# Gathering the routed rows of an expert in float32 by a scaled selection, and using the freed memory for a quarter of a down-projection chunk

## The reference

```python
logits = h2 @ w_router + b_router
top_v, top_i = lax.top_k(logits, 4)
gates = softmax(top_v)
# for each expert e, over the rows (tokens) that chose it:
gu = xb @ w_gate_up[e] + b_gate_up[e]              # 1024 -> 2048
gate, up = minimum(gu[:, :1024], 7), clip(gu[:, 1024:], -7, 7)
act = (up + 1) * gate * sigmoid(1.702 * gate)
yb = act @ w_down[e] + b_down[e]                   # 1024 -> 1024
y[row_tok] += yb * row_g
```

## Time and profile before

| | |
|---|---|
| median of 3 executions | 1183.34 us (1183.27 to 1184.69) |
| profiled execution, its own time | 1185.5 us |
| its span in the profile | 1183.7 us |
| TensorE busy | 1133.4 us, 96% |
| VectorE, ScalarE busy | 381.9 us, 181.8 us |
| mean DMA rate | 375 GB/s over the span |

### The profile page before, as it was taken

One profiled execution on the slowest core, in us unless ns is written; L12 is line 12 of the kernel. 1 busy time (PEld: TensorE's weight loads), 2 busy tenths in 40 slices (PEclk: granted clock), 3 DMA queues, 4 the chain that ended last, 5 costly groups with the idle time before them and its releaser, 6 DMA issues.

```text
span 1183.7 us, 18704 instructions
## 1 busy us (share of the span) xinstructions
PE 1133.4 (96%) x7502; PEld 573.7 (48%) x7503; DVE 381.9 (32%) x891; ACT 181.8 (15%) x395; POOL 21.6 (2%) x65
## 2 busy tenths in 40 slices
PE   8999999999999999999999999999999999999996
PEld 7989889855443433344333333333333333333342
DVE  5888878455221111222211111111111111111112
ACT  4611521343100000000000000000000000000002
POOL 3000010000000000000000000000000000000000
PEclk9999999999999999999999999999999999999999
DMA  9954204989999999999999999999999999999995
GB/s 314 373 176 144 73 10 153 345 330 393 420 427 429 435 430 428 434 431 430 437 427 433 434 427 435 432 429 436 429 433 435 426 435 431 430 435 424 424 425 221
DMA packets 41353, 444.24 MB, mean 375 GB/s; under 512 B 4270, under 2 KB 5656, under 8 KB 24540
## 3 DMA queue, kind: packets, MB, share of 16 engines
q1 hardware_dynamic: 39868, 440.45, 88.8%
q0 software_dynamic: 480, 1.85, 0.6%
q10 hardware_dynamic: 960, 1.31, 0.4%
HBM read 442.55 MB, written 1.05 MB: 375 GB/s over the span
## 4 chain that ended last, share of the span: by engine, by line
PE 65%; DMA 31%; SPq 2%; DVE 1%; ACT 0%; issue 0%; DVEq 0%; ACTq 0%
DMA ring<-in_w_gate_up 30%; PE bank L1180 22%; PE bank L1171 13%; PE bank L736 7%; PE bank L732 4%; PE bank L1210 4%; PE bank L1225 3%; DMA ring<-in_w_in 1%; PE bank L715 1%; PE bank L1107 1%; PE bank L1296 1%; PE bank L1201 1%; SPq L490 1%; PE bank L1287 1%; PE bank L913 1%; PE bank L1019 1%
## 5 line engine op out<-in xcount | busy, mean ns | idle before, releaser
L1180 PE MATMUL bank<-ring,region 128*64 128x512 f32 x2048 | 464.2, 608 | 36.3 <-DMA ring<-in_w_gate_up 36.2
L1180 PEld LDWEIGHTS bank<-ring,region 128*64 128x64 f32 x2048 | 147.0, 140 | 333.9 <-issue 268.4
L1171 PE MATMUL bank<-ring,region 128*64 128x512 f32 x1024 | 226.8, 595 | 0.3 <-ACT region L1419 0.3
L2328 DVE TENSOR_SCALAR region<-bank 128x512 f32<-128x512 f32 x32 | 22.1, 692 | 574.2 <-PE bank L1180 574.2
L1171 PEld LDWEIGHTS bank<-ring,region 128*64 128x64 f32 x1024 | 71.1, 137 | 130.1 <-issue 127.2
L1419 ACT ACTIVATE region<-bank 128x256 f32<-128x256 f32 (+1 forms) x130 | 53.3, 437 | 366.9 <-PE bank L1171 251.1
L1419 ACT ACTIVATE bank<-region 128x512 f32<-128x512 f32 x32 | 19.2, 601 | 452.9 <-DVE region L2328 452.9
L736 PE MATMUL bank<-ring 128*128 128x256 f32 x392 | 86.6, 380 | 0.0
L736 PEld LDWEIGHTS bank<-ring 128*128 128x128 f32 x392 | 73.8, 190 | 10.9 <-issue 0.7
L1210 PE MATMUL bank<-region 64*128 64x512 f32 x264 | 65.6, 615 | 0.1
L1225 PEld LDWEIGHTS bank<-region,r_levels 128*128 128x128 bf16 x1536 | 61.2, 117 | 1.6 <-issue 1.6
(11 more groups left out here) (318 smaller groups left out, 772.3 us busy)
## 6 DMA issues: line engine op xcount, KB each, us to landing
ring<-in_w_gate_up SPq DMA_DIRECT2D x48, 4096.0 KB, 30.2
ring<-in_w_down SPq DMA_DIRECT2D x24, 4096.0 KB, 36.9
ring<-in_w_gate_up SPq DMA_DIRECT2D x26, 2048.0 KB, 14.8
ring<-in_w_down SPq DMA_DIRECT2D x10, 2048.0 KB, 13.5
ring<-in_w_in SPq DMA_DIRECT2D x6, 2048.0 KB, 19.2
ring<-in_w_gate_up SPq DMA_DIRECT2D x11, 1024.0 KB, 35.2
ring<-in_w_xkv SPq DMA_DIRECT2D x4, 2048.0 KB, 11.2
ring<-in_w_down SPq DMA_DIRECT2D x7, 1024.0 KB, 8.7
```

Of the source, the lines that this page charges most:

```text
L1171: last = pe.matmul(bk[half * ROWS:(half + 1) * ROWS, :], lhs, w[:, half * 512:(half + 1) * 512], start=start, stop=stop, skip_group_check= ...
L1180: last = pe.matmul(rows, lhs, columns[:, half], start=start, stop=stop, skip_group_check=True)
L2328: v.tensor_scalar(g_t, bank_g[:, :], LIMIT, None, ALU.min).then_inc(sem["g_clamped"], 1)
```

## The change

- The three bfloat16 parts, `cut`, `rest`, `sel`, `row_scales`, `scales`, `keep_warm` and `scale_xb` go. `h2` stays in `r_levels` as float32 (8 KB a partition).
- A gather has `scaled_sel` (float32, 128 tokens x 64 rows, scaled by the norm factor) as weights and h2 streaming past it, 512 columns at a time, the two halves to partitions 0-63 and 64-127 of `bank_a`: 2 halves x 2 token halves, 4 products. The rows come out by token: ScalarE copies them to SBUF (`take_rows`, into the place of `g_t`), TensorE turns them with four transposes (`turn_rows`), VectorE copies them to `xbT` (`take_turned`).
- In a block the gather stands ahead of the scatter, the turning behind `comb`; in the last block they stand after chunk 0 and at the end. In the first block everything is gathered before the first product, copied and turned in two halves; `bias_of(bank_u)` moves behind chunk (0, 1).
- The freed 4 KB a partition, `spare`, takes the first quarter of chunk (1, 5) as soon as the squares that used the place are done; the rest of (1, 5)'s first half is what its slot still loads. Chunk (1, 4) comes in four parts instead of three: 256 KB of its last quarter is loaded once the third half-square is done, the last 256 KB once the first block's rows are turned. The `seed` copies come earlier in ScalarE's order.

```diff
-        act_t = u_t
+        act_t, rows_t = u_t, g_t
...
-        left_over = region10[:, D:2 * D]
-        half_squares = r_t[:, 2 * D + HALF:3 * D]
-        h2_parts = r_t[:, :].bitcast(BF16).rearrange("p (i t n) -> p i t n", i=3, t=NT)
+        half_squares, lead_rows_t = region10[:, D:D + HALF], region10[:, D + HALF:2 * D]
+        h2 = tm(r_t)
+        spare = r_t[:, 2 * D:3 * D]
...
             load_cols(1, 3, 0, D)
+            sp.wait_ge(sem["x1_squared"], NT)
+            sp.dma_start(spare, source(*SPARE)[:, 0:D]).then_inc(sem["spare_in"], 16)
             wait_full(sp, "xo01")
             load_chunk(1, 1)
+            sp.wait_ge(sem["x2_squared"], 3)
+            load_cols(1, 4, 3 * D, SLOT - HALF)
             sp.wait_ge(sem["seeded"], NT)
             load_cols(1, 4, 0, D)
...
-            sp.wait_ge(sem["cut_ready"], CUTS * len(PIECES))
-            load_cols(1, 4, 3 * D, SLOT)
+            sp.wait_ge(sem["lead_turned"], 2)
+            load_cols(1, 4, SLOT - HALF, SLOT)
...
-                    load_cols(e, k, 0, SLOT // 2)
+                    load_cols(e, k, D if (e, k) == SPARE else 0, SLOT // 2)
...
+            def gather(t):
+
+                for half in range(2):
+                    last = pe.matmul(bank_a[half * ROWS:(half + 1) * ROWS, :], scaled_sel[:, t, :], h2[:, t, half * HALF:(half + 1) * HALF],
+                                     start=(t == 0), stop=(t == NT - 1), skip_group_check=True)
+            def turn_rows(src, bk, tiles):
+
+                for a in tiles:
+                    last = pe.matmul(bk[:, a * P:(a + 1) * P], src[:, a * P:(a + 1) * P], ident[:, :], start=True, stop=True,
+                                     is_transpose=True, skip_group_check=True)
...
+            pe.wait_ge(sem["scaled_ready"], 1)
+            pe.wait_ge(sem["xw_ready"], len(PIECES))
+            gather(1).then_inc(sem["lead_rows"], 1)
...
+            pe.wait_ge(sem["lead_taken"], 1)
+            turn_rows(lead_rows_t, bank_u, range(0, 2)).then_inc(sem["lead_turned"], 1)
+            pe.wait_ge(sem["lead_taken"], 2)
+            turn_rows(lead_rows_t, bank_a, range(2, 4)).then_inc(sem["lead_turned"], 1)
...
-                        if final and k < 2:
-                            next_rows(k)
-                        if lead and k == 0:
-                            pe.wait_ge(sem["cut_ready"], len(PIECES) * CUTS)
-                            gather_half(range(KT // 2, KT), 1).then_inc(sem["xb_psum"], 1)
+                        if final and k == 0:
+                            next_rows()
                         if lead and k == 1:
+                            bias_of(bank_u, D, False)
...
+                    if not final:
+                        next_rows()
                     scatter_and_combine()
                     if not final:
-                        next_rows(0)
+                        turn_next_rows()
...
-                    if not final:
-                        next_rows(1)
-                        pe.wait_ge(sem["actT_rest"], w1)
-                        pe.wait_ge(sem["scaled_ready"], pe.snap(w1 + 1))
-                        scales().then_inc(sem["xb_psum"], 1)
...
+                act.wait_ge(sem["rows_psum"], w1)
+                act.wait_ge(sem["sig_ready"], w1)
+                act.wait_ge(sem["u_clamped"], act.snap(2 * w1))
+                take_rows(rows_t, slice(0, ROWS_PER)).then_inc(sem["rows_taken"], 1)
 
                 act.wait_ge(sem["comb_psum"], w1)
                 fn(combT, bank_d[:, 0:T], ACT.Copy).then_inc(sem["comb_ready"], 1)
...
-                dve.wait_ge(sem["xb_psum"], dve.snap(w1 + 1))
-                v.tensor_copy(row_scales, bank_g[:, 0:ROWS]).then_inc(sem["rs_ready"], 1)
-                dve.wait_ge(sem["rs_ready"], dve.snap(w1 + 1))
-                scale_xb(0, KT, sem["xb_ready"])
+                dve.wait_ge(sem["xb_psum"], w1)
+                take_turned(bank_a, 0, 4, sem["xb_ready"])
```

More of the change, by code:

```diff
@@ L1181, in pair_of_inner, with bias_of @@
                 return last
[L1183 to L1195, removed]
-                return last
-            def scales(halves=range(NT)):
-                for t in halves:
-                    last = pe.matmul(bank_g[:, 0:ROWS], all_ones, scaled_sel[:, t, :], start=(t == 0), stop=(t == NT - 1))
+            def bias_of(bk, c0, first=True):
+                pair_of_inner(bk, one_hot, b_gu[:, c0:c0 + D], first, False)
+            def gather(t):
+                for half in range(2):
+                    last = pe.matmul(bank_a[half * ROWS:(half + 1) * ROWS, :], scaled_sel[:, t, :], h2[:, t, half * HALF:(half + 1) * HALF],
+                                     start=(t == 0), stop=(t == NT - 1), skip_group_check=True)
+                return last
+            def turn_rows(src, bk, tiles):
+                for a in tiles:
+                    last = pe.matmul(bk[:, a * P:(a + 1) * P], src[:, a * P:(a + 1) * P], ident[:, :], start=True, stop=True,
+                                     is_transpose=True, skip_group_check=True)
                 return last
@@ L1213, in scatter @@
                         last.then_inc(signal, 1)
[L1215 to L1226, removed]
-                return last
-            pe.wait_ge(sem["cut_ready"], 2 * CUTS)
-            gather_half(range(KT), 0)
+                return last
+            pe.wait_ge(sem["xw_ready"], 2)
+            gather(0)
             pe.wait_ge(sem["gu_part_ready"], 3)
@@ L1268, in one_time, with expert, next_rows, turn_next_rows @@
                 pe.matmul(first_of_psum, first_col, spans, start=True, stop=True).then_inc(sem["blocks_psum"], 1)
[L1270 to L1274, removed]
+            def expert(e, slots, counts, last_tiles={}, lead=False, final=False, by_halves=False, in_spare=False):
+                def next_rows():
+                    pe.wait_ge(sem["scaled_ready"], pe.snap(w1 + 1))
+                    for t in range(NT):
+                        last = gather(t)
+                    last.then_inc(sem["rows_psum"], 1)
+                def turn_next_rows():
+                    pe.wait_ge(sem["rows_taken"], w1)
+                    turn_rows(rows_t, bank_a, range(4)).then_inc(sem["xb_psum"], 1)
                 def scatter_and_combine():
@@ L1322, in expert @@
                             f = k * GU_TILES + a
-                            if lead and (f, bk) == (KT // 2, 0):
+                            if lead and (f, bk) == (2, 0):
                                 pe.wait_ge(sem["xb_rest"], 1)
@@ L1327, in expert @@
                             c = a * 2 * D + bk * D
-                            last = pair_of_inner((bank_g, bank_u)[bk], xbT[:, f, :], wk[:, c:c + D], False, f == KT - 1)
+                            last = pair_of_inner((bank_g, bank_u)[bk], xbT[:, f, :], wk[:, c:c + D], lead and (f, bk) == (0, 1),
+                                                 f == KT - 1)
                             if (f, bk) == (KT - 1, 0):
@@ L1705, in _, with take_rows @@
             taken(fn(h2T[:, 6:8, :], tiles("eT11", P)[:, 2:4, :], ACT.Copy), "eT11")
-            cut(4, 0)
             seed(1, 1, "eT11")
             gate_exps(1)
-            cut(4, 1)
-            cut(4, 2)
+            def take_rows(dst, tiles):
+                c = slice(tiles.start * P, tiles.stop * P)
+                return fn(dst[:, c].rearrange("p (a i) -> p a i", i=P),
+                          bank_a[:, :].rearrange("p (i a) -> p a i", a=ROWS_PER)[:, tiles], ACT.Copy)
+            act.wait_ge(sem["lead_rows"], 1)
+            for a in (0, 2):
+                take_rows(lead_rows_t, slice(a, a + 2)).then_inc(sem["lead_taken"], 1)
             act.wait_ge(sem["gT_psum"], 1)
@@ L2458, in _ @@
                 e, rows = bass.ds(e_of, 1), iota[:, bass.ds(row_of, ROWS)]
-                select(e, rows)
                 select_scaled(e, rows)
```

94 lines of the change are left out of this document (21 added, 73 removed).

## The result

The changed kernel takes **1186.40 us** (median of 14 runs, 1185.22 to 1189.88) beside 1184.51 us for the kernel before (14 runs, 1183.21 to 1188.39): ratio **1.0018, 95% interval 1.0010 to 1.0027**. It is slower by some 2 us, not 0.6 us faster. (The kernel before was itself 1.17 us slower here than the 1183.34 us of its first three executions, so 1.2 of the 3.7 us between the 1182.7 us forecast and the result are not the change's.) Its profiled execution took 1187.58 us, with a span of 1185.8 us.

What follows compares the result with a forecast made beforehand. The weights' DMA stream was taken to bound the experts, tied to slots TensorE frees. From the profiled 1185.5 us, preload -0.1, fetches -0.7, end +0.2 gave 1184.9; the median lies 2.16 lower: 1182.7 us, range 1180.4 to 1185.2.

Steps and rivals of the forecast that it cites:

- These places decide: Slot-bound loads at (2, 0), (4, 2) and expert 3's end: stream gains only as margins of 2.3, 3.1, 2.9 us allow.
- The end of expert 3, with its 2.9 us: Loads of (5, 2) and (5, 3): 2.8 us late against margin 2.9, so 0.1 us of the preload passes.
- the hole that was expected near 387 us: Sign at expert 3's end: DMA engines idle near 387 us, where the preload is nearly all given back.
- Later TensorE gains 3 us an expert on the stream, so loads are issued ever earlier and the margins only grow: Experts after the listed loads: TensorE gains 3 us an expert, so later slot-bound loads would not decide.
- The first block, 0.8 us late: Expert 0's start: one selection less, but gather, copies and turning added; first product at 279.6 us, 0.8 us later.
- A block, +0.5 us: Between gate-up and down: gather and transposes replace gathers and scales, +0.25 us, plus +0.25 for an uncovered ScalarE copy.
- that rival: Gather's halves don't overlap: 1.75 us more a block, 1189.6 us; chance of over 2.4 us slower this way 0.09.
- The clock falls in the first block: Rival: without `keep_warm` TensorE idles around the ranks and its clock drops, costing 1.7 us; 1184.3 us, chance 0.12.
- Nothing at all to the stream: Rival: quarter preloaded but next load starts at the old time, fetches fall yet lag as much; 1183.5 us, chance 0.15.
- The fetches, 0.7 us: Expert stream: a quarter fewer instruction fetches, and engines starting level after an idle time, gain 0.7 us, bounds 0 and 1.6.
- The end, +0.2 us: Last block: `take_rows`, the transposes and the gather in one piece add 0.2 us after the last load.
- The last block does not wait for its tile: Sign in the last block: its 0.42 us wait for a load should remain; its absence would show the prediction wrong.

Runs made afterwards that it cites:

- e7: Kernel before with the useless `keep_warm` product run six times instead of once ahead of the first block, 2.1 us once: ratio 1.0017.
- e6: Kernel before with the scale products of every block but the last made twice, 0.45 us more TensorE time a block: ratio 1.0023.
- e4: Changed kernel without the preload of the quarter of (1, 5), last quarter of (1, 4) in one piece; 5 runs: ratio 1.0035.
- e2: Changed kernel with cover: turning of the next rows moved behind turning of the activations, so TensorE works during ScalarE's copies: ratio 1.0011.
- e5: Kernel before with the scale products of every block but the last made four times, 1.34 us more TensorE time a block: ratio 1.0090.
- e8_change_again: The changed kernel run once more, nothing altered, against the kernel before: ratio 1.0026.
- e8_no_preload_again: Changed kernel without the preload, run once more beside the repeated change: ratio 1.0025 to the kernel before.
- e9: Changed kernel with warming (two unused products around the ranks) and cover (turning moved behind the activations' turning), without the preload: ratio 1.0002.
- e10: Changed kernel with warming, cover and preload, and chunks (2, 0) and (2, 1) loaded by halves: ratio 0.9996 to the kernel before.
- e3: Changed kernel with both warming (two unused products around the ranks) and cover (turning moved behind the activations' turning), preload kept: ratio 1.0002.
- e1: Changed kernel with warming: two unused products in TensorE's waits before and after the ranks: ratio 1.0017 to the kernel before.

## Why the prediction was wrong

**The picture held, and the result lay outside.** The stream bounds the experts, a load is tied to the slot that TensorE frees, and TensorE's lateness decides how much of the preload passes. The sum went wrong in two steps on that lateness.

**"These places decide", with margins of 2.3 and 2.9 us**: the terms that failed. The last part of (1, 4) and the halves of (1, 5) come before both and were given no margin; e7 shows 0 us there. At (2, 0) the margin of 2.3 us was about 0 too: in the repeat of the change it is issued at 287.22 us, 0.34 us later than before from the top-8 (0.4 forecast), so 1.9 us of the preload should have passed, and none did (78 GB/s less over 8 us are 1.44 us, 12 less over 20 us 0.56, for 1.25 us gained ahead).

The landing of 296.1 us that the margin was taken from is that of the slowest of 16 engines. In the completion records of the same trace the first engine was done with that load at 293.9 us, where a load into an idle queue would have been done at 293.8: what the slowest engine lags behind was counted as room, while by this sum the first one had nothing left to do. At expert 6 the same sum gives 3.75 us by the last engine (478.86) and 0.1 by the first (475.19); e6 found 1.2 to 1.4. So the landing of the last engine is only an upper bound.

The end of expert 3, with its 2.9 us, does not decide at all. Its load is issued at 387.47 us in the changed kernel, 3.35 us late for 2.8 forecast, and the hole that was expected near 387 us is not there: 442 and 434 GB/s over the 20 us from 374.61, for 449 and 426 before.

**"Later TensorE gains 3 us an expert on the stream, so loads are issued ever earlier and the margins only grow"**: the other one. The function `slot_of` deals the nine pairs of chunks of a body of three experts round five couples of slots and starts anew with the next body, so the first pairs of a body wait for slots that were used four pairs before, not five. The first such load is that of (8, 0) and (8, 1), at the end of expert 6: issued at 463.11 before and at 467.16 after. Its room is the 1.4 us or less of e6; the changed kernel is 3.3 to 4.7 us late there. From one body to the next the sentence holds: the same load at the end of expert 9 is issued at 541.47 us before and at 546.88 after, 6.04 us late, and the stream has no hole there (439 and 435 GB/s over the 15 us from 540.24 and 539.61).

```profile
463.11 0.33 SPq L474 DMA_DIRECT2D ring<-in_w_gate_up  x1
```

is SP's queue before, and after:

```profile
467.16 0.33 SPq L472 DMA_DIRECT2D ring<-in_w_gate_up  x1
```

**The first block, 0.8 us late**: 1.12 in the profile of the change, 1.01 in its repeat (first product at 280.09 us, top-8 at 275.53). The selection ended 1.95 us after the top-8 for 2.12 before, the 0.2 us less that was forecast; TensorE's 0.75 us in front of the gather are nearly all the wait for it. From its end to the first product it was 2.72 us for 2.4: the first gather with its hand-over to ScalarE took 1.12 us for 0.96, and from the turning's start to VectorE's copy it was 0.59 us for 0.44.

**A block, +0.5 us**: measured 26.47 or 26.61 us from one down projection's start to the next, for 26.12 before: +0.35 to +0.49. The gather's 8 records took 1.72 us (1.75 expected), the turning 0.44 (0.56), and the uncovered copy some 0.4 (0.25). The halves run side by side; that rival is out.

**The clock falls in the first block**, chance 0.12: it did, in the profile taken, and cost 1.24 us (8.33 for 7.09) for 1.7 expected. It did so again in e4's profile, and not in those of both repeats and of e2, with the same first block. That `keep_warm` went is not what it hangs on: e5, whose first block is the kernel before's with `keep_warm` in it, shows a fall too, from 277.4 us on, with 0.53 us idle ahead of the ranks as its longest wait there.

In the medians the clock can be part of the 0.25%: of 12 executions each, 5 of the change (e8_change_again) and 4 without the preload (e8_no_preload_again) had a mean granted clock of 0.984 or less, and the medians of the others are 0.7 and 0.8 us lower; of the 24 with warming and cover timed beside them (e9, e10) none had, of the 35 of the kernel before 4. Where in those executions the clock was lower no trace shows.

**Nothing at all to the stream**, chance 0.15: the preload's half of this is what came true. e9 beside e3 shows that the loads start early and later loads wait as much longer.

**The fetches, 0.7 us**: their number fell by a quarter as said. DMA queue view, 282 to 1170 us, of the changed kernel:

```profile
q8 instruction: 11, 0.18, 0.1%
```

15 before. But the stream gained nothing by it: from the landing of the load at the end of expert 6 (15.7 us after its issue before, 14.3 after) to the end of the same wait of TensorE in block 30 (1125.22 and 1128.02) it is 646.4 and 646.6 us. The Trainium skill, Runtime: NRT & Kernel Launch, Instruction fetch mechanics, calls the cost of crossing a block of instructions "mostly hidden". This stretch holds one of the 15 packets before and none after, so it weighs neither that nor the 0.7 us, and no run here does.

**The end, +0.2 us**: nothing of it shows. Timeline of the changed kernel:

```profile
1164.37 1.99 PE L1208 MATMUL bank<-region 64*128 64x512 f32 x8
...
1167.56 7.09 PE L1173 MATMUL bank<-ring,region 128*64 128x512 f32 x32 [0.31 <-ACT region L1407]
```

From the scatter's start to the down projection 3.19 us both times (1162.25 to 1165.44 before), and from there to the end of the span 18.2 us, 18.3 before. The last block does not wait for its tile, which the prediction named as a sign that it was wrong.

**What it comes to.** Without the preload the kernel is 0.25% slower, and a dose of 0.45 us a block gives 0.23% by lateness alone. Of the 0.0025, the cover and the warming together take back 0.0023 (e9 beside e8_no_preload_again, timed together, intervals apart), 2.7 us, of which 1.5 us at the hole of expert 6 (380 GB/s became 423 over 15 us). Another 0.8 us may be the executions with the lower mean clock, as said above; that is a count of executions and not an experiment. How the two edits share it stays open, since the intervals of e1, e2 and e3 overlap.

## What to carry to other kernels

When a ring of slots feeds a stream, TensorE's time is free only up to the room of the tightest slot. List the places where a slot is used again soonest (a pattern of slots that starts anew in a loop has one in each turn), and measure the room with a dose: repeat a harmless instruction and see from what lateness on the DMA rate falls. Look first at the very first loads that wait for something. A lateness counts only as far as the stream is not late itself. Work that an instruction did as cover for another engine's copy belongs to the cost of taking it out; here moving one line behind the transposes took back 2.5 us of lateness by expert 6 (3.33 to 0.81).

## What the runs showed of the hardware

- A load lands with its slowest engine, and the engines drain apart: in the kernel before the 16 completions of (2, 0) lie between 293.90 and 296.10 us, those of the 4 MB load issued at 463.11 us between 475.19 and 478.86. The load of the earlier trace rows that took 9.5 us from issue took 8.7 us in the changed kernel, issued 1.69 us later from the top-8, with holes in the stream ahead of it.
- The same program at the same place shows the clock fall in one profiled execution and not in the next (granted 0.60 from 278 to 280 us in the changed kernel, no fall in its repeat), with TensorE idle in the same pieces of 0.43, 0.75 and 0.23 us. With two products of no use, 0.49 and 0.70 us long, none of four profiles has a fall (e1, e3, e9, e10); of the ten without them three have one (the changed kernel, e4, e5).
